# Two transformer blocks on one core: the second block's mixing stage on unscaled x, with the token factor in the evictions

## What is computed

```python
h = rmsnorm(x, gain)                       # h = x * gain / sqrt(mean(x^2) + eps), one factor per token
z = h @ w_in                               # 6308 columns, split into
uv, p, q, k, v, q_idx, k_idx, w_idx, ab, gates = split(z)
y0 = gmlp_mixer(uv)                        # gelu, norm, causal 128x128 product over tokens
y1 = pool_mixer(p)                         # running means over 2, 4, 8, 16 tokens
y2 = sparse_attention(q, k, v, q_idx, k_idx, w_idx)   # index scores choose 64 keys per query
y3 = conv_mixer(ab)                        # a * sigmoid(gt), depthwise convolution of 31 taps, layer norm, silu
mixed = sum(sigmoid(gates[i]) * (y[i] @ w_branch[i]) for i in range(4))
x = x + rmsnorm(mixed @ w_out, post_gain)
```

## Time and profile before

| | us |
|---|---|
| median of 3 runs | 1923.51 (1923.35 to 1923.55) |
| the profiled execution | 1923.3 |
| its span, first to last instruction | 1921.6 |
| PE busy | 1911.6 (99%) |
| VectorE busy | 1384.7 (72%) |
| ScalarE busy | 928.5 (48%) |
| GpSimd busy | 220.9 (11%) |

### The profile page before, as it was taken

One profiled execution on the slowest core, in us unless ns is written; L12 is line 12 of the kernel. 1 busy time (PEld: TensorE's weight loads), 2 busy tenths in 40 slices (PEclk: granted clock), 3 DMA queues, 4 the chain that ended last, 5 costly groups with the idle time before them and its releaser, 6 DMA issues.

```text
span 1921.6 us, 28027 instructions
## 1 busy us (share of the span) xinstructions
PE 1911.6 (99%) x11022; PEld 1676.8 (87%) x11022; DVE 1384.7 (72%) x1596; ACT 928.5 (48%) x1032; POOL 220.9 (11%) x187
## 2 busy tenths in 40 slices
PE   9999999999999999999999999999999999999998
PEld 7999888889998888888898888888888898888887
DVE  7776766667677666766769777667766769777666
ACT  6564443445644344644555546435544554545443
POOL 0000000000001000000049320000000049320000
PEclk9999999999999999999999999999999999999999
DMA  7544555554356555455554555555555554555553
GB/s 280 196 154 163 190 187 186 195 193 174 135 188 211 184 192 197 177 187 190 179 176 143 197 197 181 192 196 175 208 183 188 175 187 138 192 197 181 183 194 109
DMA packets 50730, 353.24 MB, mean 184 GB/s; under 512 B 6064, under 2 KB 6192, under 8 KB 9040
## 3 DMA queue, kind: packets, MB, share of 16 engines
q1 hardware_dynamic: 47952, 341.93, 49.8%
q0 software_dynamic: 2400, 9.99, 1.5%
q10 hardware_dynamic: 288, 0.05, 0.0%
HBM read 349.85 MB, written 2.10 MB: 183 GB/s over the span
## 4 chain that ended last, share of the span: by engine, by line
PE 98%; DVE 1%; issue 0%; DMA 0%; ACT 0%; DVEq 0%; POOLq 0%; POOL 0%; SPq 0%; ACTq 0%
PE ps L230 21%; PE ps L305 11%; PE ps L306 11%; PE ps L313 11%; PE ps L235 11%; PE ps L208 5%; PE ps L215 5%; PE ps L209 5%; PE ps L190 3%; PE ps L192 3%; PE ps L191 3%; PE ps L2674 1%; PE ps L2679 1%; PE ps L2675 1%; PE ps L2383 1%; PE ps L1317 1%
## 5 line engine op out<-in xcount | busy, mean ns | idle before, releaser
L166 DVE TENSOR_TENSOR w_lo<-raw,w_hi 128x2048 fp32r<-128x2048 f32 x317 | 728.9, 2303 | 270.4 <-ACT w_hi L159 269.6
L159 ACT ACTIVATE w_hi<-raw 128x2048 fp32r<-128x2048 f32 x317 | 607.0, 1917 | 466.3 <-PE ps L313 220.5
L230 PE MATMUL ps<-a,w_hi 128*128 128x512 f32 x1792 | 428.0, 390 | 1.2 <-DVE a L431 1.0
L230 PEld LDWEIGHTS ps<-a,w_hi 128*128 128x128 f32 x1792 | 332.7, 188 | 70.9 <-DVE a L431 2.8
L305 PE MATMUL ps<-w_hi,mixH 128*128 128x512 f32 x848 | 332.5, 392 | 0.0
L306 PE MATMUL ps<-w_hi,mixL 128*128 128x512 f32 x848 | 331.1, 390 | 0.0
L235 PEld LDWEIGHTS ps<-a,w_lo 128*128 128x128 f32 x1792 | 229.8, 191 | 8.7
L235 PE MATMUL ps<-a,w_lo 128*128 128x256 f32 x1792 | 232.4, 283 | 0.0
L313 PE MATMUL ps<-w_lo,mixH 128*128 128x512 f32 x848 | 209.5, 389 | 0.0
L313 PEld LDWEIGHTS ps<-w_lo,mixH 128*128 128x128 f32 x848 | 159.2, 188 | 33.0
L305 PEld LDWEIGHTS ps<-w_hi,mixH 128*128 128x128 f32 x848 | 159.5, 188 | 32.2 <-ACT b_gates L1878 0.8
(11 more groups left out here) (406 smaller groups left out, 2359.5 us busy)
## 6 DMA issues: line engine op xcount, KB each, us to landing
raw<-in_w_b SPq DMA_DIRECT2D x198, 1024.0 KB, 4.8
raw<-in_w_a SPq DMA_DIRECT2D x124, 1024.0 KB, 4.8
rows<-in_post_gains POOLq DMA_DIRECT2D x6, 512.0 KB, 4.0
rows<-in_rows_a POOLq DMA_DIRECT2D x2, 1028.0 KB, 7.1
raw<-in_w_a SPq DMA_DIRECT2D x4, 512.0 KB, 6.9
x<-in_x SPq DMA_DIRECT2D x2, 512.0 KB, 5.4
bias_line<-a_gates POOLq DMA_DIRECT2D x1, 1024.0 KB, 4.8
out<-x SPq DMA_DIRECT2D x4, 256.0 KB, 2.0
```

Of the source, the lines that this page charges most:

```text
L159: act.activation(k.w_hi[:, s, :], k.raw[:, s, :], ACT.Copy).then_inc(k.hi_ready, 1)
L166: dve.tensor_tensor(k.w_lo[:, s, :], k.raw[:, s, :], k.w_hi[:, s, :].bitcast(F32), ALU.subtract).then_inc(k.lo_ready, 1)
L230: pe.matmul(both, hi[:, kt, n * P:(n + 1) * P], k.a[:, :, kt, :], start=kt == 0, stop=False)
```

## The change

In the mixing stage of both layers of the second block, all products take x * gain without the token factor. The scaling of x, its second set of transposes and the eviction into nH, nL go. The token factor goes into the evictions: the six feature chunks (3 to 8) are made with `f_pair` and evicted by VectorE with a sum and a product with `r_rows`, where ScalarE evicted them before; the gates' tanh takes half the factor as its scale. The factor is spread by a product with ones behind feature 3 (bank 7) and copied by ScalarE. The tanh of the GLU's gate reads the scaled eviction from SBUF. Three splits move: high 2 into the norm, high 3 and low 2 ahead of the wait for the factor. y0's transposes go to bank 7, and the wait for its split moves ahead of the index products, which write this bank. The y's take the buffer of nH, nL, and the mixed result that of aH, aL. The diff, cut to its core:

```diff
@@ PE: mixing stage, per layer
-                for b in range(4):
-                    if b % 2 == 0:
-                        pe.wait_ge(scaled0.sem, scaled0.at(l, b // 2 + 1))
-                        pe.wait_ge(scaled1.sem, scaled1.at(l, b // 2 + 1))
-                    for kk in range(2):
-                        for tt in range(TT):
-                            kt = 2 * b + kk
-                            ins = pe.transpose(k.ps[:, 4 + b, kk * SEQ + tt * P:kk * SEQ + (tt + 1) * P],
-                                               xs[:, tt, kt * P:(kt + 1) * P], k.ident)
-                    ins.then_inc(nT_done.sem, 1)
...
-                    f_chunk(k, pe, M0 + i, st.count(l, M0 + i), [3 if i == 5 else i % 2], [range(8)], nop)
+                    if i == 4:
+                        pe.wait_ge(f_evicted.sem, f_evicted.at(l, 1))
+                    elif i in (5, 6):
+                        pe.wait_ge(s_evicted.sem, s_evicted.at(l, i - 4))
+                    elif i == 8:
+                        pe.wait_ge(s_evicted.sem, s_evicted.at(l, 4))
+                    f_pair(k, pe, M0 + i, mixed_bank[i], st.count(l, M0 + i))
 
                 feature(3)
+                pe.wait_ge(diag_ready.sem, diag_ready.at(l, 2))
+                for tt in range(TT):
+                    ins = pe.matmul(k.ps[:, 7, tt * P:(tt + 1) * P], ones, diag[:, tt, :], start=True, stop=True)
+                ins.then_inc(rbc_done.sem, 1)
...
-                    t_late(k, pe, M0 + i, st.count(l, M0 + i), range(4 * half, 4 * half + 4), 512, nop,
+                    t_late(k, pe, M0 + i, st.count(l, M0 + i), range(4 * half, 4 * half + 4), 512, aop,
...
-                pe.wait_ge(f_evicted.sem, f_evicted.at(l, 4))
+                pe.wait_ge(s_scaled.sem, s_scaled.at(l, 4))
+                pe.wait_ge(y0_split.sem, y0_split.at(l, 1))
...
-                pe.wait_ge(f_evicted.sem, f_evicted.at(l, 6))
-                pe.wait_ge(y0_split.sem, y0_split.at(l, 1))
+                pe.wait_ge(s_scaled.sem, s_scaled.at(l, 6))
                 scores(1)
@@ ScalarE
-                norm_in(l, 1)
-                high.upto(M0 + 2)
+                norm_in(l, 1, lambda: high.upto(M0 + 2))
+                high.upto(M0 + 3)
                 act.wait_ge(rstd_ready.sem, rstd_ready.at(l, 2))
-                for h in range(2):
-                    cols = slice(h * DM // 2, (h + 1) * DM // 2)
-                    act.activation(xs[:, 0, cols], k.x[:, 0, cols], ACT.Copy, scale=rho[:, 0:1]).then_inc(scaled0.sem, 1)
...
+                high.upto(M0 + 5)
+                act.wait_ge(rbc_done.sem, rbc_done.at(l, 2))
+                act.activation(r_rows, k.ps[:, 7, 0:SEQ], ACT.Copy).then_inc(rbc_ready.sem, 1)
                 high.upto(M0 + 6)
-                act.wait_ge(k.chunk_done, st.results(l, M0 + 4))
-                act.activation(flat(conv_y[:, :, :]), k.ps[:, 0, :], ACT.Tanh, scale=0.5).then_inc(f_evicted.sem, 1)
-                high.upto(M0 + 7)
...
+                act.wait_ge(s_scaled.sem, s_scaled.at(l, 2))
+                act.activation(flat(conv_y[:, :, :]), flat(conv_y[:, :, :]), ACT.Tanh, scale=0.5).then_inc(glu_ready.sem, 1)
                 high.upto(M0 + 8)
...
-                            act.activation(gates_t[:, tt, g // 2, g % 2, :], k.ps[:, (6, 0)[g % 2] + tt, :], ACT.Tanh, scale=0.5)\
+                            act.activation(gates_t[:, tt, g // 2, g % 2, :], k.ps[:, (6, 0)[g % 2] + tt, :], ACT.Tanh,
+                                           scale=half_rho[:, tt:tt + 1])\
@@ VectorE
+                low.upto(M0 + 2)
                 dve.wait_ge(rstd_ready.sem, rstd_ready.at(l, 2))
...
+                dve.tensor_scalar(half_rho, rho, 0.5, None, ALU.mult).then_inc(half_ready.sem, 1)
+                for tt in range(TT):
+                    ins = dve.tensor_scalar(diag[:, tt, :], k.ident, rho[:, tt:tt + 1], None, ALU.mult)
+                ins.then_inc(diag_ready.sem, 1)
...
+                def evict(i, dst):
+
+                    dve.wait_ge(k.chunk_done, st.results(l, M0 + i))
+                    dve.tensor_reduce(dst, halves(k, mixed_bank[i]), AX.X, ALU.add).then_inc(s_evicted.sem, 1)
+                    dve.wait_ge(s_evicted.sem, s_evicted.at(l, i - 2))
+                    dve.tensor_tensor(dst, dst, mid(r_rows, 2), ALU.mult).then_inc(s_scaled.sem, 1)
+
+                hc = conv_x[:, :, CONV_PAD:]
+                dve.wait_ge(rbc_ready.sem, rbc_ready.at(l, 2))
+                evict(3, hc)
...
                 low.upto(M0 + 6)
...
+                evict(4, conv_y[:, :, :])
+                low.upto(M0 + 7)
+                dve.wait_ge(glu_ready.sem, glu_ready.at(l, 1))
+                dve.wait_ge(s_scaled.sem, s_scaled.at(l, 1))
+                dve.scalar_tensor_tensor(hc, conv_y[:, :, :], 1.0, hc, ALU.add, ALU.mult).then_inc(hc_ready.sem, 1)
+                evict(5, pz[:, :, POOL_PAD:])
...
-                conv_taps(3)
+                conv_taps(1)
+                evict(6, idxF[:, :, :])
+                dve.wait_ge(y0H_ready.sem, y0H_ready.at(l, 1))
+                dve.tensor_tensor(flat(yL[:, 0:2, :]), k.ps[:, 7, :], flat(yH[:, 0:2, :]).bitcast(F32), ALU.subtract)\
+                   .then_inc(y0_split.sem, 1)
+                low.upto(M0 + 9)
+                evict(7, qkF[:, 0:2, :])
+                conv_taps(2)
...
+                evict(8, qkF[:, 2:4, :])
                 low.upto(M0 + 10)
@@ GpSimd
-                pool.wait_ge(f_evicted.sem, f_evicted.at(l, 3))
+                pool.wait_ge(s_scaled.sem, s_scaled.at(l, 3))
@@ buffers
+        mixed_bank = {3: 4, 4: 0, 5: 4, 6: 0, 7: 2, 8: 0}
-        yH, yL = k.aH, k.aL
+        yH, yL = k.mix[:, 0], k.mix[:, 1]

```

More of the change, by code:

```diff
@@ L1799, in norm_in @@
                 x_square(l, n, 0)
+                if meanwhile is not None:
+                    meanwhile()
                 x_high(l, n, 1)
@@ L1859, in _ @@
-                act.activation(flat(idxF[:, :, :]), k.ps[:, 0, :], ACT.Copy).then_inc(f_evicted.sem, 1)
                 act.wait_ge(y0T_done.sem, y0T_done.at(l, 1))
-                act.activation(flat(yH[:, 0:2, :]), k.ps[:, 3, :], ACT.Copy).then_inc(y0H_ready.sem, 1)
+                act.activation(flat(yH[:, 0:2, :]), k.ps[:, 7, :], ACT.Copy).then_inc(y0H_ready.sem, 1)
                 high.upto(M0 + 9)
-                for i in range(2):
-                    act.wait_ge(k.chunk_done, st.results(l, M0 + 7 + i))
-                    act.activation(flat(qkF[:, 2 * i:2 * i + 2, :]), k.ps[:, 1 - i, :], ACT.Copy).then_inc(f_evicted.sem, 1)
-                    if i == 0:
-                        act.wait_ge(rel_done.sem, rel_done.at(l, 1))
-                        for h in range(IH):
-                            ins = act.activation(rel[:, h, :], k.ps[:, 4 + h, 0:3 * P], ACT.Relu, scale=ID ** -0.5)
-                        ins.then_inc(rel_ready.sem, 1)
-                    high.upto(M0 + 10 + i)
+                act.wait_ge(rel_done.sem, rel_done.at(l, 1))
@@ L1873, in gate_in @@
+                for h in range(IH):
+                    ins = act.activation(rel[:, h, :], k.ps[:, 4 + h, 0:3 * P], ACT.Relu, scale=ID ** -0.5)
+                ins.then_inc(rel_ready.sem, 1)
+                high.upto(M0 + 11)
                 def gate_in(i):
@@ L2159, in _ @@
                 low.upto(M0 + 8)
-                dve.wait_ge(y0H_ready.sem, y0H_ready.at(l, 1))
-                dve.tensor_tensor(flat(yL[:, 0:2, :]), k.ps[:, 3, :], flat(yH[:, 0:2, :]).bitcast(F32), ALU.subtract)\
-                   .then_inc(y0_split.sem, 1)
-                low.upto(M0 + 9)
                 def conv_taps(n):
@@ L2673, in branch @@
                         for kk in range(4):
-                            pe.matmul(out[kk // 2], k.aH[:, 4 * q + kk, cols], hi[:, kk, :], start=kk % 2 == 0, stop=False)
-                            pe.matmul(out[kk // 2], k.aL[:, 4 * q + kk, cols], hi[:, kk, :], start=False, stop=False)
+                            pe.matmul(out[kk // 2], yH[:, 4 * q + kk, cols], hi[:, kk, :], start=kk % 2 == 0, stop=False)
+                            pe.matmul(out[kk // 2], yL[:, 4 * q + kk, cols], hi[:, kk, :], start=False, stop=False)
                         if tt == 0:
@@ L2678, in branch @@
                         for kk in range(4):
-                            ins = pe.matmul(out[kk // 2], k.aH[:, 4 * q + kk, cols], lo[:, kk, :], start=False, stop=kk % 2 == 1)
+                            ins = pe.matmul(out[kk // 2], yH[:, 4 * q + kk, cols], lo[:, kk, :], start=False, stop=kk % 2 == 1)
                         if tt == 0:
@@ L2716, in _ @@
                     pe.wait_ge(mix_split.sem, mix_split.at(l, i + 1))
[L2717 removed]
+                    t_late(k, pe, WO + i, st.count(l, WO + i), range(2 * i, 2 * i + 2), DM, aop, t_out, i == 0, False,
                            between=(lambda: mixed_transpose(1)) if i == 1 else None)
                 wait_mixed(2)
[L2720 removed]
```

(4 more changed lines are left out.)

76 lines of the change are left out of this document (21 added, 55 removed).

## The result

The kernel after takes 1929.66 us (median of 9 runs, 1928.48 to 1932.74) against 1923.51 of the kernel before: a ratio of 1.0033, with a 95% interval of 1.0025 to 1.0042. It is slower by some 6 us, where 1928.4 us was forecast and 1923.0 to 1933.0 was the range. The profiled execution took 1930.83 us around a span of 1928.3 us.

The account below looks back on a forecast made before the run. VectorE was to become the bound up to chunk 17: 0.8 + 1.6 + 0.6 = 3.0 us late, less 0.47 slack, 2.5 per layer; 1923.3 + 5.1 = 1928.4 us, range 1923.0 to 1933.0.

Parts of the forecast that it names:

- PE's gain: Mixing stage: 1.66 us from removed transposes plus 1.6 from six feature chunks, less 0.45 for the factor spread, 2.8 per layer.
- Chunk 7's chain: VectorE's scaled gate, then ScalarE's tanh (0.5 us) and high half (1.9): chunk 7 ready for its low half at 990.2.
- rival C: Faster: PE stays the bound and takes its 5.7 us, 1917.6, if VectorE passes chunk 17 2.3 us earlier; chance 0.08.
- The lock: VectorE's four added scalings (5 to 8) wait for GpSimd's instructions: 0 to 3.9 us per layer, 1.6 taken.
- Rival B: No measurable change: scalings fall into GpSimd's gaps, VectorE late by 0.5 to 2.4 us at chunk 17; chance 0.34.
- walk: VectorE's steps after chunk 7 is ready at 990.2, summing to 28.1 us: top-k search starts at 1018.3, 0.8 later.
- The tail: GpSimd's convolution ends later, so VectorE's last taps before chunk 17 run under it: 0 to 1.3 us, 0.6 taken.
- PE's waits: PE stands some 1.7 us ahead of the attention scores, the rest ahead of low halves of gates 15 to 17.
- Each wait has only PE's own rest behind it: Mixing stage: ScalarE's high halves and SP's loads follow VectorE's low halves by the same distance and add nothing to PE's waits.
- A: The forecast: VectorE bounds from chunk 10 to 17 under GpSimd's lock, over 3.85 us slower in both layers; chance 0.56.
- the three taps: VectorE's step of 3.58 us between eviction 7 and the scores, ahead of the top-k search.

Follow-up runs that it names:

- e10: Changed kernel with chunk 7's high half ahead of the tanh, last taps spread 0, 2, 4, 6, and chunk 8 back in 256-column products: 1919.03 us.
- e11: Changed kernel with chunk 7's high half ahead of the tanh, last taps spread 0, 2, 4, 6, and all six feature chunks in 256-column products: 1920.71 us.
- e1: Changed kernel with ScalarE making chunk 7's high half ahead of the tanh of the GLU gate instead of behind it: 1924.83 us.
- e2: Changed kernel with GpSimd's convolution taps 1 to 15 left out, so the output lacks them: 1919.25 us.
- e4: Changed kernel without the product with the row of factors in the six feature evictions, the sums kept: 1925.86 us.
- e7: Changed kernel with chunks 7 and 8 back in 256-column products summed in one PSUM bank, evicted and scaled in one VectorE instruction: 1922.81 us.
- e8: Changed kernel with all six feature chunks back in 256-column products, evicted and scaled in one VectorE instruction: 1923.92 us.
- e5: Changed kernel with VectorE's last twelve tap instructions respread round the low halves, four instead of twelve of them ahead of chunk 17's: 1924.54 us.

## Why the prediction was right, point by point

**PE's gain** was mis-sized: 2.4 us per layer, not 2.8. The transposes gave 1.75 (1.66 taken) and the spread cost 0.54 (0.45 taken). The six chunks, 33.9 us in all or 5.65 each, gave 1.2 and not 1.6: I had taken the MLP's 5.57, in which pairs follow pairs, but between the mixing chunks other products lie, and the high products right behind small ones take 3.71 to 3.80 us (980.14 to the first low product at 983.94, the longest) against 3.65 in the other two. e10 and e11 bear out the size: 0.18 per chunk, where the phases give 5.84 - 5.65 = 0.19. The isolated spacing of the Trainium skill (TensorE: Matmul & The Clock Gate, section Back-to-back issue gap) would make it an estimated 0.04 per chunk, 16 times 2.5 ns: the trace doesn't agree with that. The row was right to decide, if not in full.

**Chunk 7's chain.** Low 7 started at 990.66 - 0.53 = 990.1, forecast 990.2. That its wait was one of the causes is shown by e1. That it would be enough to undo it (rival C's condition) is refuted by e1: there it took away the scores' wait and not gate 17's.

**The lock.** Four scalings exposed, 1.6 us taken. They took 0.80 and three times 1.44 where 0.69 is undisturbed: 0.11 + 3 x 0.75 = 2.4 us. e2 shows the cause: without GpSimd's additions the three take 0.69, and the first stays at 0.80 beside the one tap that GpSimd still weighs. So "two thirds of the time, some 0.4 each" was the weakest number; three of four paid the same 0.75. Ahead of two of the three, GpSimd's weighing had itself run longer beside VectorE (3.25 us at 997.39 and 3.97 at 1002.08, where its shortest is 1.83), ended within the 1.2 us of VectorE's sum, and its addition started before the scaling did: 1000.61 and 1006.02 against 1001.02 and 1006.43. The third met its addition as well (1016.57, 1016.95). Rival B had argued the opposite, that the sum lets GpSimd finish. The search was to start 2.4 us later and was 2.5: a larger lock and a walk that was some 0.6 too long cancelled. The Trainium skill (SBUF — State Buffer, section SBUF: two separate sides) has the lock for a whole instruction, and the trace agrees: the low half of chunk 17 started 0.13 us behind an addition of 1.37 and was 1.1 longer.

**The tail** is the part that failed, though it doesn't show in the total. 0.6 was taken for the taps ahead of chunk 17, and they took 5.9 us for 5.5 (before's row, up to 1061.24):

```profile
1055.77 5.55 DVE L2175 SCALAR_TENSOR_TENSOR conv_y<-conv_x,rows,conv_y 128x256 f32<-128x256 f32 x8
```

But low 17 itself, which the working had at its undisturbed length, was longer by 1.1. That would make 2.5 + 0.5 + 1.1 = 4.1 us at chunk 17, and it was 2.6. The rest is a second step that the prediction left out: the old order paid the lock too, in the mask behind the search, and the new one pays less of it there. VectorE's timeline of before, two products of the mask:

```profile
1041.96 2.36 DVE L2244 TENSOR_TENSOR RL<-RL,keep 128x1024 f32<-128x1024 f32 x1
...
1047.88 1.79 DVE L2244 TENSOR_TENSOR RL<-RL,keep 128x512 f32<-128x512 f32 x1
```

and the same two of after:

```profile
1045.20 1.24 DVE L2243 TENSOR_TENSOR RL<-RL,keep 128x1024 f32<-128x1024 f32 x1
...
1050.56 0.68 DVE L2243 TENSOR_TENSOR RL<-RL,keep 128x512 f32<-128x512 f32 x1
```

They are 2.2 us shorter in after. Between the search and chunk 17 other rows change as well: two of the mask are 1.1 and 0.5 longer, a low half behind the search is 0.8 shorter (3.05 at 1021.86 before); the sum of these is 1.4 us less, which leaves 2.7 of the 4.1. A lock added in one place is in part a lock moved from another.

**PE's waits.** 1.4 ahead of the scores (1.7 forecast), 0.5 at gate 16, 2.1 at gate 17, none at 15. A wait costs more than its row: in the second layer the distances between the starts grow by 1.52, 0.77 and 2.42 us against e10's, 4.7 in all where the rows name 4.05, since the products right behind a wait are slower. 4.7 - 2.4 = 2.3 us per layer, forecast 2.5. "Each wait has only PE's own rest behind it" held for the other engines' work and not for PE's: the products behind a wait are part of its price. Two layers make 4.6, which with before's 1921.6 is 1926.2; the three runs of after in which the mean clock was 1.000 had spans of 1926.4 to 1926.8.

**What was missing** is the rest, 2.1 us in the profiled execution, whose span is 1928.3. 0.5 of it is the distance with which this trace reaches the stage, and 1.6 lie behind a wait. The view by windows of after, behind the first layer's wait at gate 17 (us of the window, busy PE, PEld, DVE, ACT, POOL, granted clock, DMA share, GB/s), and the same place of the second layer:

```profile
1067.60:1069.30 1.70, 1.70 (x6) 1.28 (x5) 1.70 (x5) 0.00 (x0) 0.00 (x0) 0.56 0.93 226
1069.30:1071.00 1.70, 1.70 (x10) 1.69 (x8) 1.70 (x3) 0.00 (x0) 0.00 (x0) 0.50 0.93 390
1071.00:1073.00 2.00, 2.00 (x18) 2.00 (x18) 2.00 (x4) 1.48 (x1) 0.00 (x0) 0.94 0.00 0
1641.00:1651.00 10.00, 7.86 (x48) 6.62 (x47) 10.00 (x12) 3.78 (x5) 2.36 (x2) 1.00 0.31 107
```

The granted clock was at 0.50, the level of 1.2 GHz, for 3.4 us, worked out from these shares: 1.5, 1.7 and 0.2 in the three windows. PE had stood for 2.13 us and then worked for 1.1 us at the full clock. The low half of gate 17 and the product with the values took 6.15 us there (1066.67 to 1072.82) and 4.55 in the second layer (1645.65 to 1650.20), whose wait was the same length and whose clock stayed at 1.00. So the forecast's 1928.4 is near the median partly by a cost that it didn't have: its own terms come to 1926.2 + 1.7 = 1927.9 us by what they measured, and the median stands 1.8 higher, by this clock and by the time outside the span. The hit is luck to that extent: PE's gain taken 0.4 per layer too large, the lock 0.8 too small, the walk 0.6 too long, low 17's lock and the mask's left out, and no price for the clock.

**The rivals.** A's condition, late by 2.4 us or more at chunk 17, held narrowly, with 2.6. B's condition, scalings in GpSimd's gaps, held for one of the four. C's price was 1917.6. e2, with nobody in PE's way, has a span of 1916.7, which with before's 1.7 beside it makes 1918.4: off by the 0.8 by which PE's gain was too large. C needed a quiet GpSimd, or another order. What I hadn't seen is how cheap that order was. The prediction names "the three taps" and the high half behind the tanh as steps of the walk, and takes their places as given.

## What to carry to other kernels

When a change shortens the engine that bounds and loads one that runs beside it, follow the second engine to the last place where the first needs it, and ask of each operation ahead of that place who needs it and when: here twelve tap instructions that nobody awaited stood ahead of a weight chunk that PE awaited, and one moved split and eight moved tap instructions turned 6 us of loss into 2.5 of gain. Time saved far upstream reaches that place only in part (e4, e7, e8): much of it turns into waiting for the next input. A microsecond saved on an engine counts in full only between its last wait and the deadline.

## What the runs showed of the hardware that was not expected

- **A wait can cost the clock behind it, or not.** The same wait of 2.1 us was followed by 3.4 us at the 1.2 GHz level in one layer and by none in the other. Kernels with such waits spread widely (e4 10.6 us, e1 6.1, e7 5.1, after 4.3, with mean clocks of 0.996 to 1.000), those with waits of 1.4 us or less hardly (e5 1.5, e8 0.8, e10 0.6). That it is the 2.1 us wait that makes the spread is consistent over the kernels and wasn't tested by itself.
- **GpSimd's lock is paid in places, not as a rate.** A product of two 512-element SBUF tensors took 0.69, 0.80, 0.92 or 1.44 us (after and e1), a low half anything from 2.28 to 3.39, by where GpSimd's addition of 1.4 us was; of after's eight low halves from 1018 to 1063 seven are at 2.28 and one at 3.39. Removing work ahead shifts what is hit: e4 has a low half of 3.10 us at 1028.12 where after has none. An instruction with one tensor input is hit as well: the mask's first, 128x384, took 0.35 us in before (1040.90) and 1.46 in after (1042.87), beside an addition that had started at 1040.92.
- **The same program falls on either side of it** (e7's two layers; in e1 the eight tap instructions take 6.01 us in the first and 4.88 in the second, and PE's waits at gate 17 are 2.14 and 0.99 us), which a reading of one layer doesn't tell.
